# The order of the expert gathers: 40 rows of U ahead, V one rank behind, scores head by head, an earlier load of w_out

## What is computed

```python
q = (xb @ w_query).reshape(PEER_BLOCK, PEER_HEADS, 2, PEER_QDIM // 2)
s = jnp.einsum('thpd,hpnd->thpn', q, sub_keys)
sv, si = lax.top_k(s, PEER_TOPK)
...
top_s, pos = lax.top_k(cand, PEER_TOPK)
idx = jnp.take_along_axis(cidx, pos, axis=-1)
gate = jax.nn.softmax(top_s.astype(jnp.float32), axis=-1)
act = jax.nn.gelu(jnp.einsum('thkd,td->thk', expert_u[idx], xb).astype(jnp.float32))
return jnp.einsum('thk,thkd->td', (gate * act).astype(xb.dtype), expert_v[idx])
```

## Time and profile before

| | us |
|---|---|
| median of three runs (2109.19 to 2114.4) | 2111.76 |
| the profiled execution | 2114.55 |
| its span, first to last instruction | 2112.7 |
| PE busy | 1682.9 (80%) |
| DVE busy | 1103.6 (52%) |
| POOL busy | 676.7 (32%) |
| ACT busy | 395.7 (19%) |

### The profile page before, as it was taken

One profiled execution on the slowest core, in us unless ns is written; L12 is line 12 of the kernel. 1 busy time (PEld: TensorE's weight loads), 2 busy tenths in 40 slices (PEclk: granted clock), 3 DMA queues, 4 the chain that ended last, 5 costly groups with the idle time before them and its releaser, 6 DMA issues.

```text
span 2112.7 us, 13926 instructions
## 1 busy us (share of the span) xinstructions
PE 1682.9 (80%) x4609; PEld 786.5 (37%) x4609; DVE 1103.6 (52%) x1840; ACT 395.7 (19%) x1142; POOL 676.7 (32%) x577
## 2 busy tenths in 40 slices
PE   4569999999799879798777777777777777777776
PEld 1134644555534567433222232323222223222222
DVE  0156877333355267135556556556557566466443
ACT  1120100212300100222122122122123122222111
POOL 1011001000000033446354354454353554454431
PEclk7789999999899999999999999999999999999999
DMA  9987778331377469699999999999999999999996
GB/s 345 390 311 279 288 259 296 105 116 60 135 272 269 142 263 352 267 407 424 423 423 423 424 423 423 423 423 423 423 422 423 423 423 423 424 423 423 424 423 255
DMA packets 144806, 723.54 MB, mean 342 GB/s; under 512 B 10185, under 2 KB 10393, under 8 KB 77666
## 3 DMA queue, kind: packets, MB, share of 16 engines
q0 software_dynamic: 92784, 614.83, 70.9%
q1 hardware_dynamic: 51792, 107.78, 14.2%
q10 hardware_dynamic: 162, 0.08, 0.0%
HBM read 720.52 MB, written 2.13 MB: 342 GB/s over the span
## 4 chain that ended last, share of the span: by engine, by line
DMA 42%; PE 32%; DVE 13%; POOL 8%; issue 3%; SPq 2%; ACT 1%; DVEq 0%; ACTq 0%; POOLq 0%
DMA ring<-in_expert_u,acc 23%; PE ps L712 11%; DMA qh<-in_expert_u,acc 8%; PE ps L838 5%; POOL ring L370 5%; PE ps L875 5%; DMA ring<-in_w_mod 4%; DVE ring L1255 3%; PE ps L706 3%; PE ps L897 3%; DMA ring<-in_expert_v,acc 2%; DMA ring<-in_w_query 2%; DMA modrow<-in_expert_v,acc 1%; PE ps L765 1%; POOL VX L370 1%
## 5 line engine op out<-in xcount | busy, mean ns | idle before, releaser
L897 PE MATMUL ps<-ring,wg 128*128 128x512 f32 x1184 | 550.8, 611 | 171.4 <-DMA ring<-in_expert_v,acc 171.4
L1255 DVE SCALAR_TENSOR_TENSOR ring<-ring,A 128x2048 f32<-128x2048 f32 x174 | 396.9, 2291 | 332.4 <-DMA ring<-in_expert_u,acc 332.1
L897 PEld LDWEIGHTS ps<-ring,wg 128*128 128x128 f32 x1184 | 218.6, 193 | 502.5 <-issue 279.7
L370 POOL DMA_INDIRECT ring<-in_expert_u,acc x174 | 223.4, 1284 | 446.8 <-DVE ring L1255 335.7
L897 PE MATMUL ps<-H,wg 128*128 128x512 f32 x576 | 265.3, 604 | 84.3 <-DMA H<-in_expert_v,acc 84.3
L600 ACT ACTIVATE wg<-K,VX 128x128 f32<-128x128 f32 x256 | 102.8, 402 | 714.0 <-PE ps L897 712.9
L712 PE MATMUL ps<-ring,H 128*128 128x512 f32 x512 | 228.2, 605 | 4.7 <-DMA ring<-in_w_in 3.5
L370 POOL DMA_INDIRECT ring<-in_expert_v,acc x148 | 175.9, 1188 | 67.5 <-issue 43.0
L897 PEld LDWEIGHTS ps<-H,wg 128*128 128x128 f32 x576 | 104.5, 191 | 244.5 <-issue 128.7
L921 DVE SCALAR_TENSOR_TENSOR acc<-ring,vec,acc 128x512 f32<-128x512 f32 x240 | 180.5, 752 | 10.9 <-DMA ring<-in_w_mod 2.5
L897 PE MATMUL ps<-modrow,wg 128*128 128x512 f32 x288 | 131.9, 601 | 39.5 <-DMA modrow<-in_expert_v,acc 39.5
(11 more groups left out here) (215 smaller groups left out, 1251.9 us busy)
## 6 DMA issues: line engine op xcount, KB each, us to landing
ring<-in_w_mod POOLq DMA_DIRECT2D x32, 2048.0 KB, 8.6
ring<-in_w_mod SPq DMA_DIRECT2D x16, 2048.0 KB, 19.7
ring<-in_w_in SPq DMA_DIRECT2D x16, 2048.0 KB, 9.2
ring<-in_w_out SPq DMA_DIRECT2D x8, 2048.0 KB, 11.0
ring<-in_w_query SPq DMA_DIRECT2D x8, 2048.0 KB, 8.6
ring<-in_expert_u,acc POOLq DMA_INDIRECT x174, 26.2
ring<-in_expert_v,acc POOLq DMA_INDIRECT x148, 27.1
B<-in_ctx SPq DMA_DIRECT2D x2, 1024.0 KB, 19.3
```

The lines of the kernel that those rows point to most:

```text
L370: nc.gpsimd.indirect_dma_start(rows_, None, table, bass.IndirectOffsetOnAxis(ap=eidx[:, rank:rank + 1], axis=0)).then_inc(loaded, 16)
L897: ins = mm(ps[:, 4 * b + n, :], diag[:, r % 4, :], v_rows[r % V_SLOTS][:, n * CH:(n + 1) * CH], start=k == 0, stop=k == BLOCK_RANKS - 1, s ...
L1255: v.scalar_tensor_tensor(out=rows_u, in0=rows_u, scalar=1.0, in1=A[:, r // BLOCK_RANKS, :], op0=ALU.mult, op1=ALU.mult, accum_out=dots[:, ...
```

## The change

- LEAD becomes 40 and LAG becomes 1. The dots from rank 20 on no longer wait for all scores.
- In the first chunk PE makes the queries of head 0, its scores, then the queries of head 1 and its scores. In the later chunks the scores are made and read by head or by pair of heads. `pick` waits for its own head's scores, and reads them where they lie (the copy to `stage` is gone).
- `soft_of(2)` and `soft_of(3)` go to the query stage; `norm_soft(0)` to `norm_soft(2)` stand before dot 32, and for g from 3 on `norm_soft(g)` stands in the middle of group g itself, where `norm_soft(g + 1)` stood.
- The scratch `tmp` moves out of the weight buffers, and SP's wait for `y_ready` is gone.

```diff
-LEAD = 20
-LAG = 4
+LEAD = 40
+LAG = 1
...
-PICK_STEPS = 24
+PICK_STEPS = 23
...
+def scores_read(head, b):
+
+    return TB * head + b + 1 if head < 2 else 4 * (head // 2) + 2 * b + 2
...
-        tmp = ringf[:, 0:4 * D]
+        tmp = Hf[:, 0:4 * FW]
...
-            sp.wait_ge(S["y_ready"], 1)
             for base, src in ((32, w_out[0]), (40, w_query[0])):
...
             for r in range(LEAD):
                 gather_u(r)
             pool.wait_ge(S["w_free"], 48)
-            pool.wait_ge(S["score_psum"], 8)
+            pool.wait_ge(S["score_psum"], TB * PH)
...
+            for head in range(PH):
+                n, i = head // 2, head % 2
+                if head == 0:
+                    act.wait_ge(S["q_psum"], 1)
+                else:
+                    act.wait_ge(S["w_free"], 40 + 2 * (n + 1))
+                nc_a.copy(qh[:, n % 2, 2 * i:2 * i + 2, :],
+                          ps[:, 2 * (n % 2) + i, :].rearrange("p (j t) -> p j t", j=2)
+                          ).then_inc(S["q_free"], 1)
+                if head >= 2 and i == 0:
+                    continue
                 for b in range(TB):
-                    act.wait_ge(S["score_psum"], TB * n + b + 1)
-                    o = b * 2 * PH * NK + n * CH
-                    nc_a.copy(sc[:, o:o + CH], ps[:, 4 + 2 * (n % 2) + b, :]
-                              ).then_inc(S["score_ready"], 1)
-                if n == 2:
+                    act.wait_ge(S["score_psum"], TB * head + b + 1)
+                    first = head if head < 2 else head - 1
+                    o = (b * PH + first) * 2 * NK
+                    size = (head + 1 - first) * 2 * NK
+                    c0 = (first % 2) * 2 * NK
+                    nc_a.copy(sc[:, o:o + size], ps[:, 4 + 2 * (n % 2) + b, c0:c0 + size]
+                              ).then_inc(S["score_ready"], head + 1 - first)
+                if head == PH - 1:
+                    soft_of(3)
+                if head == 5:
                     soft_of(0)
                     soft_of(1)
+                    soft_of(2)
...
-                    if r % TOPK == 3 and 2 <= g + 1 < TB * PH:
+                    if r % TOPK == 3 and 4 <= g + 1 < TB * PH:
                         soft_of(g + 1)
...
+            for kh in range(2):
+                pe.wait_ge(w_ld[kh], 16 * 13)
+                query(0, kh, 0)
+                ins = query(0, kh, 1)
+            ins.then_inc(S["q_psum"], 1)
+            score(0)
+            for kh in range(2):
+                query(0, kh, 2)
+                query(0, kh, 3).then_inc(S["w_free"], 1)
+            score(1)
+            for n in range(1, 4):
...
+                score(2 * n)
+                score(2 * n + 1)
...
-                sq = tmp[:, 4096 + b * FW:4096 + (b + 1) * FW]
+                sq = tmp[:, 2048 + b * FW:2048 + (b + 1) * FW]
...
-                step(v.tensor_copy(stage, sc[:, g * (2 * NK):(g + 1) * (2 * NK)]))
+                head, b = g % PH, g // PH
+                dve.wait_ge(S["score_ready"], scores_read(head, b))
+                scores = sc[:, g * (2 * NK):(g + 1) * (2 * NK)]
...
-            dve.wait_ge(S["score_ready"], 1)
             pick(0, 0)
             pick(1, 1)
             for g in range(TB * PH):
                 for r in range(TOPK):
                     if g == 0 and r == TOPK // 2:
-                        dve.wait_ge(S["score_ready"], 3)
                         pick(2, 2)
-                    if g == 1 and r == LEAD - TOPK:
-                        dve.wait_ge(S["score_ready"], 8)
+                    if g == 2 and r == 0:
                         norm_soft(0)
                         norm_soft(1)
-                    if 2 <= g + 1 < TB * PH and r == TOPK // 2:
-                        norm_soft(g + 1)
+                        norm_soft(2)
+                    if g >= 3 and r == TOPK // 2:
+                        norm_soft(g)
                     dot(g * TOPK + r)
```

More of the change, by code:

```diff
@@ L183, in build @@
         xtmp = QTf[:, 0:2 * CH]
-        stage = QTf[:, 0:2 * NK]
         cand, work = QTf[:, 256:512], QTf[:, 512:768]
@@ L209, in build @@
         g2_ready o_sig hsq out_free x1_ready ssq2 std2 h2_ready h2T_psum h2T_ready keys_psum
-        keys_ready q_free score_psum score_ready u_free pair_free
+        keys_ready q_psum q_free score_psum score_ready u_free pair_free
         diag_ready exp_ready soft_ready bank_done ssq3 std3 final_ready stored dve act""".split()
@@ L574, in soft_of @@
                                 ACT.Exp, accum_out=sums[:, g:g + 1]).then_inc(S["exp_ready"], 1)
[L576 to L581, removed]
-                for b in range(TB):
-                    act.wait_ge(S["score_psum"], TB * n + b + 1)
-                    o = b * 2 * PH * NK + n * CH
-                    nc_a.copy(sc[:, o:o + CH], ps[:, 4 + 2 * (n % 2) + b, :]
-                              ).then_inc(S["score_ready"], 1)
-                if n == 2:
+            for head in range(PH):
[9 more added lines that the diff above has]
+                    continue
+                for b in range(TB):
+                    act.wait_ge(S["score_psum"], TB * head + b + 1)
[8 more added lines that the diff above has]
+                if head == 5:
                     soft_of(0)
                     soft_of(1)
+                    soft_of(2)
             def weight_of(r):
@@ L863, in _, with query, score @@
             pe.wait_ge(S["keys_ready"], 4)
-            for n in range(4):
+            def query(n, kh, j):
+                for k in range(KH):
+                    kk = kh * KH + k
+                    ins = mm(ps[:, 2 * (n % 2) + j // 2, (j % 2) * T:(j % 2 + 1) * T],
+                             W[kh][:, k, j * P:(j + 1) * P], h2T[:, kk, :],
+                             start=kk == 0 and j % 2 == 0, stop=kk == KB - 1,
+                             skip_group_check=True)
+                return ins
+            def score(head):
+                n, i = head // 2, head % 2
+                pe.wait_ge(S["q_free"], head + 1)
+                for b in range(TB):
+                    if head == 1:
+                        pe.wait_ge(S["score_ready"], TB)
+                    elif n >= 2 and i == 0:
+                        pe.wait_ge(S["score_ready"], scores_read(head - 3, b))
+                    for p_ in range(2):
+                        j = 2 * i + p_
+                        ins = mm(ps[:, 4 + 2 * (n % 2) + b, j * P:(j + 1) * P],
+                                 qh[:, n % 2, j, b * P:(b + 1) * P], keysT[:, 4 * n + j, :],
+                                 start=True, stop=True)
+                    ins.then_inc(S["score_psum"], 1)
+            for kh in range(2):
[9 more added lines that the diff above has]
+            for n in range(1, 4):
                 if n >= 2:
@@ L871, in _ @@
                     for j in range(4):
[L872 to L878, removed]
-                    ins.then_inc(S["w_free"], 1)
[L880 to L889, removed]
+                        ins = query(n, kh, j)
+                    ins.then_inc(S["w_free"], 1)
+                score(2 * n)
+                score(2 * n + 1)
+            pe.wait_ge(S["score_ready"], 4 * PH // 2)
             for r in range(RANKS):
@@ L1215, in pick @@
                 sq = lambda t: t.rearrange("p (a c) -> p a c", a=TOPK)
-                step(v.tensor_copy(stage, sc[:, g * (2 * NK):(g + 1) * (2 * NK)]))
+                head, b = g % PH, g // PH
+                dve.wait_ge(S["score_ready"], scores_read(head, b))
+                scores = sc[:, g * (2 * NK):(g + 1) * (2 * NK)]
                 for p_ in range(2):
                     ins = top16(sv[:, 16 * p_:16 * p_ + 16], siu[:, 16 * p_:16 * p_ + 16],
-                                stage[:, p_ * NK:(p_ + 1) * NK], work[:, p_ * NK:(p_ + 1) * NK])
+                                scores[:, p_ * NK:(p_ + 1) * NK], work[:, p_ * NK:(p_ + 1) * NK])
                 step(ins)
```

## The result

| | before | changed |
|---|---|---|
| median of four runs, us | 2111.77 (2109.19 to 2114.4) | 2178.61 (2177.65 to 2180.81) |
| span of the profiled execution | 2112.7 | 2178.8 |
| PE busy | 1682.9 (80%) | 1657.1 (76%) |

The changed kernel is slower by the factor 1.0314, with a 95% interval of 1.030 to 1.0327.

The account below looks back on a forecast made before the run. The prediction took full DMA engines to bound the gather stage. Its terms, -15.2 (w_out) - 29 (lead) + 87 (late norm_soft) + 1 (tail) = +44 us, turned the median 2111.76 into 2155, range 2122 to 2180.

Parts of the forecast that it names:

- The bound: Gather stage: full DMA engines set the pace at 422 to 424 GB/s, 5.0 us a rank; running dry loses time.
- norm_soft a group later: Groups 5 to 15: V 16g + 7 waits for a buffer, DMA runs dry, 8 us in each group, 87 us lost.
- The way up to V: In each stall, after U 16g + 7 lands: dot 2.35, norm_soft 0.45, weight 1.0, PE 3.7 plus 2.1, POOL's start 0.3 us.
- the clock: First rank of each stalled group: PE has stood over 25 us, runs at half clock, 2.1 us more than 3.7.
- the restart: End of each stall: 5.7 us from V's issue to its landing, of which 3.2 us are start-up.
- w_out: Ahead of the queries: loading it early hides the load and lets PE start at the upper clock, gaining 15.2 us.
- The lead: From first gather to first V: U 37 goes out 13.5 us later with 17 fewer transfers left, gaining 29 us.
- The share of `w_query` beside the gathers: In the lead: its pieces get 21% of the DMA bytes and land in 24 us, not 10.
- The hole at `pick(2)`: In the lead: pick(2) ends at 797 us, the five U buffers have run empty, DMA idles about 4 us.
- the one at `pick(3)`: In the lead: pick(3) ends at 873 us, its five U's landed at 871, DMA idles about 7 us.
- the first gather: Start of the gather stage: half the first chunk suffices, so it moves from 763.66 to 748.1, by 15.6 us.
- Tail: After the last landing: PE still trails from group 15's stall and ends 8.5 us later, before 7.4; cost 1 us.

## Why the prediction was right

**The bound** held: where the early norm_soft or LAG 4 keeps the DMA engines full, the kernel gains; where they run dry, it loses.

**norm_soft a group later** was the step that decides, and it is shown: by the place (an early norm_soft takes all of it away), by the depth (LAG 2, 3, 4), by the buffers (6 instead of 7) and by the kernel before. Eleven stalls were forecast, groups 5 to 15, eleven are in the chain. Its size was 7.9 us a group, and is 9.0: 12 of the 24 us that were missing. The way up to V was right: from the dot of U 16g + 7 to the issue of V 16g + 7 there are 9.9 us on the mean of eleven stalls (9.2 to 10.6), and the terms of the prediction after the landing make 9.9. The first rank takes 6.0 us of it on the mean, forecast 5.8, so the clock was rightly a term of the sum. The term that was too small is the restart. From the issue of V to the next dot it takes 8.9 us on the mean, where 5.7 to the first landing and 2.48 for the next transfer make 8.2. That is 0.7 of the 1.1 us; another 0.2 is a slip, since the terms add up to 50.6 - 42.5 = 8.1 and the sum goes on with 7.9.

**w_out** gained 9.65 us instead of 15.2 in this kernel, 12 alone. The step that failed is that nothing else waits: I had the load of x and w_mod as wanted only at the end of the chunk, but they seem to delay the next piece of w_out itself. POOL's two loads of w_mod go out around it:

```profile
584.97 0.90 POOL L323 DMA_DIRECT2D ring<-in_w_mod  x1 [13.93 <-issue]
590.89 0.88 POOL L323 DMA_DIRECT2D ring<-in_w_mod  x1 [5.03 <-DVE acc L957]
```

The piece of w_out was issued at 586.60, between them, and took 18.93 us by the chain of waits, where the median piece of w_out lands in 8.0 us. That the loads cause this is read from the times; no run moved them. It is 5.5 of the 24 us.

**The lead** gained 22.8 us instead of 29: U 37 went out 10.05 us after U 20 of before (871.82 against 861.77), with 17 fewer transfers of 2.5 us left, 32.4 us, of which 9.65 are w_out's. The share of `w_query` beside the gathers was right in its consequence; the page's line of these loads:

```profile
ring<-in_w_query SPq DMA_DIRECT2D x8, 2048.0 KB, 17.6
```

It says 17.6 us from issue to landing, 8.6 before. The hole at `pick(2)` and the one at `pick(3)` are both there, where the prediction has them, the second with 10 us of idle DMA engines instead of 7. The 6.2 us that were missing come about so. `pick(2)` ended 3.4 us late, because its piece of `w_query` landed 2.3 us late and PE then took 15.77 us for half a chunk instead of 14.0, at a lower clock after its wait. The 24 dots up to `pick(3)` took 66.6 us instead of 64. Three norm_softs ahead of dot 32, left out of the prediction, cost 1.0 us, and `pick(3)` itself was 1.0 us shorter than forecast. The last scores were made at 853.75, 12.6 us ahead of where the prediction put them, and it gained nothing: V 0 stood behind U 37 to U 40 in POOL's order. How much of the 22.8 us belongs to the longer lead and how much to the new order of the scores no run separates; the first gather alone came 15.3 us earlier after the start of the queries, forecast 15.6.

**Tail.** PE's last line and the last stretches of the DMA engines:

```profile
2155.05 13.90 PE L933 MATMUL ps<-ring,wg 128*128 128x512 f32 x32
```

```profile
2158.00:2162.00 4.00, 4.00 (x11) 1.79 (x10) 0.82 (x2) 2.38 (x5) 0.00 (x0) 1.00 0.50 207
2162.00:2166.00 4.00, 4.00 (x11) 1.82 (x10) 0.00 (x0) 0.00 (x0) 0.00 (x0) 1.00 0.00 0
```

The landings end at about 2160, PE at 2168.95: 8.9 us, forecast 8.5, before 7.4.

The terms so measured, -9.65 - 22.8 + 11 x 9.0 + 1.5, make +68 us; the spans differ by 66.1. The direction and the mechanism came out as forecast. All four terms missed to the same side, and that the sum of +44 us still ended within the range is in part luck.

## What to carry to other kernels

A step that runs once per group (a normalization, a scale) and on which all work of the group waits must be done before the transfers that are still queued have landed. With the late norm_soft 8 MiB in the queue (LAG 4) were enough here, 6 MiB nearly, 2 MiB not. When the distance between two streams is shortened, list everything that was hidden by it, and count in bytes still queued at the moment the blocked issuer is let go. Idle engines and low clocks ahead of that count are free; each microsecond behind it is paid once per group.

## What the runs showed that I had not expected

- POOL's gather instructions grow beside a dot. One that starts while DVE runs a dot takes 2.2 us at the median and up to 3.0 us, one that starts without a dot 0.94 us. In a full stream this is hidden. At a restart it is not: with LAG 2 the next dot came 10.9 us after V's issue where V's own instruction was the long one, against 8.9 us in the changed kernel.
- Where PE stood for 4.10 us behind 28.49 us of dense work, the first rank after it took 5.09 us, against 3.60 without the gap and 6.62 after 32.53 us. The price depends on the queue: at a dry queue each microsecond of it counted, and with LAG 4 a first rank of 5.37 us cost nothing.
